# Holding GpSimd's table, row and alibi loads back until the first weight units have landed

## The chip, the cores and the metric

The kernel runs on one core of one Trainium2 chip. The time is the device time of one execution in microseconds (us), and the figure compared is the median of the runs. The core has five engines with a queue of instructions each: TensorE (PE, matmuls and transposes), VectorE (DVE), ScalarE (ACT), GpSimd (POOL) and SyncE (SP, which here only starts DMA transfers). They wait for each other through semaphores, written `wait_ge` in the code.

## The reference

The program is a chain of six stages on 256 tokens of width 1024, all in float32: a hybrid token mixer, a gated FFN, a gMLP mixer, an MLP, a latent attention and a second MLP. The change touches the beginning only:

```python
h = rms_norm(x, mix_pre_norm[l])
mix = hybrid_token_mixer(h, w_in[l], ...)       # proj = h @ w_in; sliding window attention,
                                                # block attention, gated delta rule; @ w_out
x = x + rms_norm(mix, mix_post_norm[l])
```

## The kernel before

All weights stream through SBUF in **units** of 1 MB (128 partitions by 2048 float32). Unit u goes by an SP transfer into one of three `raw` slots (`load`, L169 to L174) and counts on semaphore `landed[u % 3]`. Float32 products are made of three matmuls on a split of each operand into a high and a low part, so a unit is first split: ACT copies `raw` into `w_hi` (`split_hi`, L184), then DVE subtracts to get `w_lo` (`split_lo`, L192) and raises `lo_ready`. A slot is loaded again once `lo_ready` says that its former unit is split. PE uses a unit in 48 matmuls (L202 to L204).

The input X (1 MB, two halves of 512 KB), then units 0, 1 and 2, then ten small parameter transfers (`params_sync`, L253 to L258), then unit 3 and so on are issued by SP in this order. ACT issues the identity matrix and the first gain. GpSimd issues what else the first stage wants: the post-norm row (`rows_load`, 512 KB), mask tables (640 KB), three tiny rows and one 64 KB row (`mix_pool`), all at once at the start, and, when the first norm's transposes are through with the buffer XN, the alibi bias (1 MB, into that same buffer).

The **first norm** goes in halves of the tokens: ACT squares X (L311), DVE adds (L340), GpSimd raises to the power -0.5 (`norm_pool`, L367), ACT and DVE scale (L315, L353), PE transposes into PSUM (L380). PE runs warm-up matmuls on the identity (L289) around this. ACT's queue then has, in order: the copy of the gain (L279), the high half of unit 0 (L184), and the high part of the normalised input hT (L332, eight pieces). DVE's queue has the low half of unit 0 (L192) and then the low part of hT (L359, eight pieces). ACT makes the fifth to eighth high piece only after the first to fourth low piece. PE's first real matmul (L202) needs low unit 0 and the first piece of hT's low part. After that ACT and DVE split units 1 and 2.

`mix_dve` waits for the alibi and for all five small loads at L1734 and L1735, ahead of the first attention scores (L910). The parameters of SP are transposed by PE at the end of unit 3. The post-norm row is used at the end of the stage (`post_dve`).

Of the kernel before, what the change touches and what calls it, by code (L numbers as in the profile page):

```python
# [57 lines left out]
def build(nc, I, out, stages):  # L58

    ctx = ExitStack()  # L60
    with ctx:
# [3 lines left out]
        def sem(name):  # L65
            return ctx.enter_context(nc.semaphore(name))
# [95 lines left out]
        landed = [sem(f"landed{s}") for s in range(RAW)]  # L162
        landed_at = [16 * sum(len(units[v][1]) for v in range(u % RAW, u + 1, RAW)) for u in range(NU)]
# [198 lines left out]
        def norm_pool(pool, n):  # L362
            if n == 0:
                pool.wait_ge(filled, 1)
            for tb in range(TB):
                pool.wait_ge(n_ms, TB * n + tb + 1)
                nc.gpsimd.tensor_tensor(stat[:, 6 + tb:7 + tb], stat[:, 4 + tb:5 + tb], mhalf[:, 0:1],  # L367
                                        ALU.pow).then_inc(n_rstd, 1)
# [47 lines left out]
        def post_pool(pool, q):  # L416
            for tb in range(TB):
                pool.wait_ge(r_ms, TB * q + tb + 1)
                nc.gpsimd.tensor_tensor(stat[:, 14 + tb:15 + tb], stat[:, 12 + tb:13 + tb], mhalf[:, 0:1],
                                        ALU.pow).then_inc(r_rstd, 1)  # L420
# [19 lines left out]
        def rows_load(pool, k, v):  # L440

            if k:
                pool.wait_ge(r_t, 4 * k)
            pool.dma_start(rows[:], v.partition_broadcast(P)).then_inc(rows_in, 16)
# [267 lines left out]
        def gmlp_pool(pool, n):  # L712
            pool.wait_ge(s_mv, TB)
            nc.gpsimd.tensor_scalar(vrs[:, :, 0], mv[:, :, 1], EPS, None, ALU.add).then_inc(s_ve, 1)
            pool.wait_ge(s_ve, 1)
            nc.gpsimd.tensor_tensor(vrs[:, :, 0], vrs[:, :, 0], mhalf[:, 0:TB], ALU.pow).then_inc(s_vr, 1)

        def gmlp_loads(pool, n):
            pool.wait_ge(x_done, 4 * (n - 1))
            pool.dma_start(wsr, I["a_w_s_2"][0].rearrange("g i j -> i g j")).then_inc(s_in, 16)  # L720
            pool.dma_start(lnr[0:GT, :], rowsof(I["a_ln_v_g_2"])).then_inc(s_in, 16)
            pool.dma_start(lnr[GT:2 * GT, :], rowsof(I["a_ln_v_b_2"])).then_inc(s_in, 16)
            pool.dma_start(bsr, I["a_b_s_2"][0].partition_broadcast(P)).then_inc(s_in, 16)
# [329 lines left out]
        def mla_loads(pool, n):  # L1053
            if n > 1:
                pool.wait_ge(x_done, 4 * (n - 1))
            pool.dma_start(mtab, I["table"][:, T_MLA:T_MLA + S + 2]).then_inc(m_in, 16)
            pool.dma_start(posi, I["positions_2"][0].partition_broadcast(P)).then_inc(m_in, 16)

        def mla_pool(pool, n):
            norm_pool(pool, n)  # L1060
            for c, (sq, width) in enumerate(((2, 256), (6, 384))):
                pool.wait_ge(m_sq, sq)
                if c == 0:
                    src = lst[:, 0:2]
                else:
                    nc.gpsimd.tensor_tensor(lst[:, 6:8], lst[:, 2:4], lst[:, 4:6], ALU.add).then_inc(m_p1, 1)
                    pool.wait_ge(m_p1, 2)
                    src = lst[:, 6:8]
                nc.gpsimd.tensor_scalar(lst[:, 8 + 2 * c:10 + 2 * c], src, 1.0 / width, EPS, ALU.mult, ALU.add).then_inc(m_p1, 1)
                pool.wait_ge(m_p1, 1 + 2 * c)  # L1070
                nc.gpsimd.tensor_tensor(lst[:, 12 + 2 * c:14 + 2 * c], lst[:, 8 + 2 * c:10 + 2 * c], mhalf[:, 0:2],
                                        ALU.pow).then_inc(m_rs, 1)
# [287 lines left out]
        def gs_(tb):  # L1360
            return slice(tb * NH, (tb + 1) * NH)
# [44 lines left out]
                at_norm(dve, gs[s - 1])  # L1406

        def mix_pool(pool, n):
            pool.dma_start(msk, I["table"][:, T_TRI:T_MLA].rearrange("p (a b) -> p a b", b=P)).then_inc(d_in, 16)
            pool.dma_start(sinkb, I["swa_sinks"][0].partition_broadcast(P)).then_inc(d_in, 16)  # L1410
            pool.dma_start(alog, I["dn_a_log"][0].partition_broadcast(P)).then_inc(d_in, 16)
            pool.dma_start(dtb, I["dn_dt_bias"][0].partition_broadcast(P)).then_inc(d_in, 16)
            pool.dma_start(dnr[:], I["dn_norm"][0].partition_broadcast(P)).then_inc(d_in, 16)
            norm_pool(pool, n)
            pool.wait_ge(n_tr, 4 * n + 4)
            pool.dma_start(alibi, I["alibi"].rearrange("p (k h s) -> p k h s", k=2, h=NH)).then_inc(d_al, 16)

            for k in range(2):
                c = slice(k * G8, (k + 1) * G8)
                pool.wait_ge(d_ss, 2 * k + 2)  # L1420
                nc.gpsimd.tensor_scalar(sse[:, c], ss[:, c], EPS, None, ALU.add).then_inc(d_se, 1)
                pool.wait_ge(d_se, k + 1)
                nc.gpsimd.tensor_tensor(ri[:, c], sse[:, c], mhalf[:, c], ALU.pow).then_inc(d_ri, 1)

            pool.wait_ge(d_la, 2)
            for lv in range(LEVELS):
                for tb in range(TB):
                    if lv:
                        pool.wait_ge(v_y, 2 * (lv - 1) + tb + 1)
                    if lv == 1:  # L1430
                        pool.wait_ge(v_u, 2 * tb + 2)
                    nc.gpsimd.tensor_tensor(Om[:, gs_(tb), :], Lm[:, gs_(tb), :],
                                            msk[:, 4 + lv, :].unsqueeze(1).to_broadcast([P, NH, P]), ALU.mult).then_inc(v_o, 1)
            pool.wait_ge(f_ss, 2)
            nc.gpsimd.tensor_scalar(ose, oss, 1.0 / DN, EPS, ALU.mult, ALU.add).then_inc(f_se, 1)
            pool.wait_ge(f_se, 1)
            nc.gpsimd.tensor_tensor(ori, ose, mhalf[:, 0:G8], ALU.pow).then_inc(f_ri, 1)
# [426 lines left out]
        posts = [st for st in stages if st in ("mix", "ffn")]  # L1864
        post_rows = {"mix": I["mix_post_norm"][0], "ffn": I["ffn_post_norm"][0]}
# [6 lines left out]
        @block.sync  # L1872
        def _(sp):
            start_sync(sp)
            for n, st in enumerate(stages):
                if st == "ffn":
                    ffn_sync(sp, passes[st])
                elif st.startswith("mlp"):
                    mlp_sync(sp, passes[st], I["mlp_w1_2"][int(st[3])], I["mlp_w2_2"][int(st[3])])
                else:  # L1880
                    for u in range(first_unit[st], last_unit[st] + 1):
                        load(sp, u)
                        if u == RAW - 1:
                            params_sync(sp)
            final_sync(sp)

        @block.gpsimd
        def _(pool):
            for n, st in enumerate(stages):
                if st in posts:  # L1890
                    rows_load(pool, posts.index(st), post_rows[st])
                if st not in ("mix", "mla"):
                    norm_pool(pool, n)
                if st == "mix":
                    mix_pool(pool, n)
                elif st == "gmlp":
                    gmlp_pool(pool, n)
                elif st == "mla":
                    mla_pool(pool, n)
                if "gmlp" in stages[n + 1:n + 2]:  # L1900
                    gmlp_loads(pool, n + 1)
                if "mla" in stages[n + 1:n + 2]:
                    mla_loads(pool, n + 1)
                if st in posts:
                    post_pool(pool, posts.index(st))
            rows_load(pool, len(posts), I["final_norm_g_2"])
            norm_pool(pool, N)
# [140 lines left out]
```

## Time and profile before

| | |
|---|---|
| Median of 3 runs | 1099.99 us (1096.3 to 1104.11) |
| Profiled execution, span from first to last instruction | 1097.3 us |
| PE busy | 1019.0 us (93%) |
| DVE busy | 630.7 us (57%) |
| ACT busy | 496.2 us (45%) |
| POOL busy | 47.5 us (4%) |
| DMA moved | 165.59 MB, mean 151 GB/s |

No time is given for the profiled execution other than its span; the median of the runs is 2.7 us above that span. Engines are PE for matmuls, PEld for PE's weight loads, DVE, ACT, POOL; SPq is the issuing of transfers by SP. L174 is line 174 of the kernel. A time ahead of an instruction is its start in us from the start of the span. The granted TensorE clock is shown as a share of 2.4 GHz, so 0.50 is the level of 1.2 GHz.

### The profile page before, as it was taken

The numbers are of one execution on the slowest core, as the hardware profiler recorded it, in microseconds if no ns is written. First come the engines' busy times: TensorE is split into PE (matmuls) and PEld (weight loads), VectorE is DVE, ScalarE is ACT, GpSimd is POOL, SyncE is SP. The second block draws the span as 40 slices with busy tenths as digits, with TensorE's granted clock in tenths as the row PEclk, the third lists the DMA queues.
The fourth block names the chain that finished last, engine by engine and source line by source line (L and its number), as shares of the span: only waits on it lengthen the run. The fifth ranks groups of instructions, "written<-read, shape, count | busy, mean of one in ns | idle before, by whom it ended". The sixth has DMA issues, their size and how long they took to land.

```text
span 1097.3 us, 16712 instructions
## 1 busy us (share of the span) xinstructions
PE 1019.0 (93%) x6895; PEld 944.5 (86%) x6895; DVE 630.7 (57%) x760; ACT 496.2 (45%) x644; POOL 47.5 (4%) x62
## 2 busy tenths in 40 slices
PE   4989979989999998999998999999889689999997
PEld 4988968779999998998997989999779578899996
DVE  3367664467666666667456655455655536554544
ACT  5355622065445555542445444444554434444442
POOL 1000132020000001000000000000000000000000
PEclk8998969999999999999999999999999799999999
DMA  8542410046555553553554655556444225555550
GB/s 283 155 154 77 154 39 1 1 135 202 184 190 191 191 180 128 158 187 111 195 172 124 218 191 191 191 181 169 137 107 154 77 76 174 192 191 191 180 165 39
DMA packets 131696, 165.59 MB, mean 151 GB/s; under 512 B 23982, under 2 KB 114539, under 8 KB 131515
## 3 DMA queue, kind: packets, MB, share of 16 engines
q1 hardware_dynamic: 130187, 160.10, 45.5%
q0 software_dynamic: 1296, 4.68, 1.4%
q8 instruction: 38, 0.62, 0.2%
q14 instruction: 15, 0.12, 0.0%
q10 hardware_dynamic: 160, 0.07, 0.0%
HBM read 163.78 MB, written 1.05 MB: 150 GB/s over the span
## 4 chain that ended last, share of the span: by engine, by line
PE 84%; DVE 7%; ACT 4%; issue 2%; DMA 1%; POOL 1%; POOLq 0%; SPq 0%; DVEq 0%; ACTq 0%
PE ps L202 26%; PE ps L203 26%; PE ps L204 25%; DMA raw<-in_w_in_dram 1%; DVE w_lo L192 1%; ACT act_tmp L311 1%; ACT w_hi L184 1%; PE ps L1546 1%; PE ps L877 1%; PE ps L1540 1%; PE ps L380 1%; ACT act_tmp L927 1%; PE ps L1551 1%; DVE union L824 1%; PE ps L887 1%
## 5 line engine op out<-in xcount | busy, mean ns | idle before, releaser
L192 DVE TENSOR_TENSOR w_lo<-raw,w_hi 128x2048 fp32r<-128x2048 f32 (+1 forms) x153 | 344.8, 2258 | 199.1 <-ACT w_hi L184 198.1
L202 PE MATMUL ps<-hT_hi,w_hi 128*128 128x256 f32 x1160 | 332.8, 287 | 10.8 <-DVE hT_lo L359 8.2
L184 ACT ACTIVATE w_hi<-raw 128x2048 fp32r<-128x2048 f32 (+1 forms) x153 | 288.6, 1887 | 114.1 <-PE ps L204 107.7
L203 PE MATMUL ps<-hT_hi,w_lo 128*128 128x256 f32 x1160 | 331.1, 285 | 0.0
L204 PE MATMUL ps<-hT_lo,w_hi 128*128 128x256 f32 x1160 | 330.6, 285 | 0.0
L202 PEld LDWEIGHTS ps<-hT_hi,w_hi 128*128 128x128 f32 x1160 | 225.6, 194 | 14.2 <-DVE w_lo L192 8.8
L203 PEld LDWEIGHTS ps<-hT_hi,w_lo 128*128 128x128 f32 x1160 | 225.5, 194 | 1.7
L204 PEld LDWEIGHTS ps<-hT_lo,w_hi 128*128 128x128 f32 x1160 | 225.4, 194 | 0.0
L202 PE MATMUL ps<-w_hi,act_hi 128*128 128x512 f32 x416 | 162.6, 391 | 0.0
L203 PE MATMUL ps<-w_hi,act_lo 128*128 128x512 f32 x416 | 162.4, 390 | 0.0
L204 PE MATMUL ps<-w_lo,act_hi 128*128 128x512 f32 x416 | 161.9, 389 | 0.0
L202 PE MATMUL ps<-w_hi,hT_hi 128*128 128x256 f32 (+3 forms) x320 | 99.1, 310 | 4.1 <-DVE hT_lo L1845 1.6
L203 PE MATMUL ps<-w_hi,hT_lo 128*128 128x256 f32 (+3 forms) x320 | 97.7, 305 | 0.0
L204 PE MATMUL ps<-w_lo,hT_hi 128*128 128x256 f32 (+3 forms) x320 | 97.6, 305 | 0.0
L204 PEld LDWEIGHTS ps<-w_lo,act_hi 128*128 128x128 f32 x416 | 78.1, 188 | 16.6
L202 PEld LDWEIGHTS ps<-w_hi,act_hi 128*128 128x128 f32 x416 | 78.4, 189 | 14.9
L203 PEld LDWEIGHTS ps<-w_hi,act_lo 128*128 128x128 f32 x416 | 78.4, 188 | 14.5
L517 ACT ACTIVATE act_tmp<-ps 128x512 f32<-128x512 f32 x40 | 23.9, 598 | 147.5 <-PE ps L204 147.5
L202 PEld LDWEIGHTS ps<-w_hi,hT_hi 128*128 128x128 f32 x320 | 62.0, 194 | 8.2 <-issue 2.1
L203 PEld LDWEIGHTS ps<-w_hi,hT_lo 128*128 128x128 f32 x320 | 62.2, 194 | 2.8 <-issue 0.2
L204 PEld LDWEIGHTS ps<-w_lo,hT_hi 128*128 128x128 f32 x320 | 62.0, 194 | 2.7
L626 DVE SCALAR_TENSOR_TENSOR act_tmp<-ps,par,act_tmp 128x255 f32<-128x255 f32 (+1 forms) x88 | 36.4, 476 | 36.1 <-ACT act_tmp L596 36.1
(270 smaller groups left out, 918.7 us busy)
## 6 DMA issues: line engine op xcount, KB each, us to landing
raw<-in_mlp_w_dram SPq DMA_DIRECT2D x64, 1024.0 KB, 5.4
raw<-in_w_up_dram SPq DMA_DIRECT2D x22, 1024.0 KB, 5.1
raw<-in_a_w_in_dram SPq DMA_DIRECT2D x16, 1024.0 KB, 5.5
raw<-in_w_in_dram SPq DMA_DIRECT2D x12, 1024.0 KB, 6.4
raw<-in_w_down_dram SPq DMA_DIRECT2D x11, 1024.0 KB, 4.9
raw<-in_a_w_out_dram SPq DMA_DIRECT2D x8, 1024.0 KB, 5.0
raw<-in_w_out_dram SPq DMA_DIRECT2D x4, 1024.0 KB, 4.9
raw<-in_b_w_o_dram SPq DMA_DIRECT2D x4, 1024.0 KB, 4.9
```

Of the source, the lines that this page charges most:

```text
L184: nc.scalar.activation(w_hi[:, s, 0:n], raw[:, r, 0:n], ACT.Copy).then_inc(hi_ready, 1)
L192: nc.vector.tensor_tensor(w_lo[:, s, 0:n], raw[:, r, 0:n], w_hi[:, s, 0:n].bitcast(F32), ALU.subtract).then_inc(lo_ready, 1)
L202: nc.tensor.matmul(o, a[0], b[0], start=start, stop=False)
L203: nc.tensor.matmul(o, a[1], b[0], start=False, stop=False)
L204: return nc.tensor.matmul(o, a[0], b[1], start=False, stop=stop)
L311: nc.scalar.activation(act_tmp[:, b, :], half(b), ACT.Square, scale=D ** -0.5, accum_out=stat[:, b:b + 1]).then_inc(n_sq, 1)
L380: mm = pe.transpose(turned(t)[:, tb * P:(tb + 1) * P], XN[:, tb, t * P:(t + 1) * P], ident[:])
L517: nc.scalar.activation(act_tmp[:, m, :], W[m][:], func).then_inc(f.t, 1)
L626: nc.vector.scalar_tensor_tensor(ys, bank[:, t * S:(t + 1) * S - back], conv_taps(j, half, t, 2 - back), ys, ALU.mult, ALU.add).then_inc(d ...
L824: nc.vector.scalar_tensor_tensor(svT[:, t, :].rearrange("p (b i) -> p b i", b=TB), ACC[t // 2 % 4][:, t % 2 * S:(t % 2 + 1) * S].rearrange ...
L877: mm = nc.tensor.matmul(o, qs[m], ks[m], start=m == 0, stop=m == len(qs) - 1)
L887: tr = pe.transpose(ACC[kb][:, h * P:(h + 1) * P], pr[:, h, kb * P:(kb + 1) * P], ident[:])
```

## The change

GpSimd now does the power step of the first norm ahead of all its loads. It then waits until unit 1 has landed and issues the table, the three tiny rows and the 64 KB row; it waits until unit 2 has landed (and, as before, until the transposes are done) and issues the alibi and, after it, the post-norm row. The loads themselves, and everything on the other engines, are the same.

```diff
         def mix_pool(pool, n):
+            norm_pool(pool, n)
+            pool.wait_ge(landed[1], landed_at[1])
             pool.dma_start(msk, I["table"][:, T_TRI:T_MLA].rearrange("p (a b) -> p a b", b=P)).then_inc(d_in, 16)
             pool.dma_start(sinkb, I["swa_sinks"][0].partition_broadcast(P)).then_inc(d_in, 16)
             pool.dma_start(alog, I["dn_a_log"][0].partition_broadcast(P)).then_inc(d_in, 16)
             pool.dma_start(dtb, I["dn_dt_bias"][0].partition_broadcast(P)).then_inc(d_in, 16)
             pool.dma_start(dnr[:], I["dn_norm"][0].partition_broadcast(P)).then_inc(d_in, 16)
-            norm_pool(pool, n)
+            pool.wait_ge(landed[2], landed_at[2])
             pool.wait_ge(n_tr, 4 * n + 4)
             pool.dma_start(alibi, I["alibi"].rearrange("p (k h s) -> p k h s", k=2, h=NH)).then_inc(d_al, 16)
+            rows_load(pool, 0, post_rows["mix"])
...
         @block.gpsimd
         def _(pool):
             for n, st in enumerate(stages):
-                if st in posts:
-                    rows_load(pool, posts.index(st), post_rows[st])
+                if st == "ffn":
+                    rows_load(pool, 1, post_rows[st])
                 if st not in ("mix", "mla"):
                     norm_pool(pool, n)
```

## Rows read from the trace of the kernel before

**Rows 1.** The page's head.
```profile
span 1097.3 us, 16712 instructions
```

**Rows 2.** The chain that ended last, 0 to 260 us: start, length, what.
```profile
1.65 14.69 DMA raw<-in_w_in_dram
16.36 1.92 ACT w_hi L184
...
21.14 0.55 PE ps L202
...
64.65 0.69 DVE act_tmp L910
```

**Rows 3.** Timeline, 0 to 24 us: start, length, engine, line, tiles, count, idle before.
```profile
4.84 0.63 ACT L311 ACTIVATE act_tmp<-X 128x512 f32<-128x512 f32 x1 [1.76 <-DMA X<-in_x_dram]
...
6.52 0.56 POOL L367 TENSOR_TENSOR stat<-stat,mhalf 128x1 f32<-128x1 f32 x1 [1.91 <-DVE stat L340]
...
9.31 0.72 ACT L315 ACTIVATE XN<-X,stat 128x512 f32<-128x512 f32 x1 [0.86 <-POOL stat L367]
...
9.94 0.15 ACT L279 COPY par<-ps 128x8 f32<-128x8 f32 x1
...
11.48 0.59 POOL L1416 DMA_DIRECT2D XN<-in_alibi_dram  x1 [2.20 <-PE ps L380]
...
18.31 2.29 DVE L192 TENSOR_TENSOR w_lo<-raw,w_hi 128x2048 fp32r<-128x2048 f32 x1 [8.51 <-ACT w_hi L184]
...
20.51 3.22 DVE L359 SCALAR_TENSOR_TENSOR hT_lo<-ps,par,hT_hi 128x256 fp32r<-128x256 f32 x8
...
21.53 0.40 SPq L174 DMA_DIRECT2D raw<-in_w_in_dram  x1
```

**Rows 4.** Timeline of ACT, 24 to 64 us (first row: from 22.58).
```profile
22.58 3.91 ACT L184 ACTIVATE w_hi<-raw 128x2048 fp32r<-128x2048 f32 x2
29.13 0.59 ACT L1618 COPY union<-ps 128x512 f32<-128x512 f32 x1 [2.65 <-PE ps L204]
...
34.89 1.18 ACT L1628 COPY union<-ps 64x512 f32<-64x512 f32 x2 [3.36 <-PE ps L204]
```

**Rows 5.** DMA issues, 0 to 8 us: count, size of each, median us to landing.
```profile
raw<-in_w_in_dram SPq DMA_DIRECT2D x3, 1024.0 KB, 19.7
```

**Rows 6.** DMA queues, 0 to 5 us: packets, MB, share (SP's and ACT's queue).
```profile
q1 hardware_dynamic: 237, 0.91, 53.8%
```

**Rows 7.** DMA queues, 6 to 8 us; q0 is GpSimd's.
```profile
q1 hardware_dynamic: 135, 0.14, 22.0%
q0 software_dynamic: 138, 0.54, 78.0%
```

**Rows 8.** DMA queues, 0 to 120 us.
```profile
q0 software_dynamic: 560, 2.30, 6.4%
```

**Rows 9.** Windows: from:to, length, busy PE PEld DVE ACT POOL (count), granted clock, DMA share, GB/s.
```profile
3.00:5.00 2.00, 0.00 (x0) 0.00 (x0) 0.00 (x0) 0.24 (x2) 1.61 (x4) 1.00 0.98 343
10.00:11.00 1.00, 0.91 (x8) 0.92 (x9) 0.00 (x0) 0.09 (x2) 0.00 (x0) 1.00 0.86 99
13.42:15.40 1.98, 0.00 (x0) 0.00 (x0) 0.00 (x0) 0.00 (x0) 0.00 (x0) 1.00 1.10 395
21.14:25.66 4.52, 4.52 (x21) 4.52 (x22) 3.75 (x8) 4.43 (x6) 0.00 (x0) 0.50 0.94 292
101.33:103.45 2.12, 0.01 (x1) 0.01 (x1) 1.40 (x2) 2.10 (x8) 0.00 (x0) 1.00 0.06 23
104.15:107.60 3.45, 3.45 (x19) 3.45 (x18) 3.10 (x7) 3.42 (x4) 0.00 (x0) 0.51 0.00 0
219.64:221.20 1.56, 0.00 (x0) 0.00 (x1) 1.29 (x2) 1.56 (x3) 0.00 (x0) 1.00 0.02 5
```

**Rows 10.** Timeline, 904.5 to 907.5 us.
```profile
905.58 0.68 POOL L444 DMA_DIRECT2D rows<-in_final_norm_g_dram  x1
905.66 0.72 ACT L315 ACTIVATE XN<-X,stat 128x512 f32<-128x512 f32 x1 [0.86 <-POOL stat L367]
905.66 0.49 DVE L353 TENSOR_SCALAR XN<-X,stat 128x512 f32<-128x512 f32 x1 [0.67 <-POOL stat L367]
```

## The prediction

> **What bounds the kernel now.** The page's head gives a span of 1097.3 us [rows 1], and I read the start through the chain that ended last, since the change moves nothing after it. The chain begins with one transfer: unit 0, issued at 1.65 us, and ACT splits it at 16.36 [rows 2]. PE's first real matmul comes at 21.14 [rows 2], 4.78 us later: high half 1.92, low half 2.29, first low piece of hT, hand-overs. From there it runs on PE; so a us saved before 21.14 is a us of the kernel, unless a later load or split cannot follow.
>
> The timeline shows that the norm is not what holds this. GpSimd's power step at 6.52 waited 1.91 us for DVE, idle from its loads by then, and ACT scaled the second half at 9.31 and copied the gain at 9.94 [rows 3]. ACT was free at 10.09 and stood until 16.36, 6.3 us, for unit 0.
>
> Now whose bytes were in the way. Up to 5 us SP's and ACT's queue had moved 0.91 MB at a total rate of 343 GB/s, and no byte of GpSimd's appears [rows 6, 9]. From 6 to 8 us GpSimd's queue took 0.54 MB and SP's 0.14 [rows 7]: weights crept at a fifth of the traffic. At 10 us the total itself fell to 99 GB/s [rows 9]. The three first units took 19.7 us in the median to land [rows 5].
>
> **The change part by part.**
>
> *The power step ahead of the loads*: nothing. It waited for DVE, not for the loads [rows 3]. X's landing gains nothing either, as GpSimd's bytes start only after 5 us, and X's first half was there at 4.84 [rows 3, 6]. Bounds: 0 to 1.76 us (ACT's whole wait for X [rows 3]) gained; I take 0.
>
> *Unit 0 without GpSimd's bytes.* The queue must move X and unit 0, 2.10 MB. 0.91 is done at 5.0 us; the other 1.19 at 343 GB/s take 3.5 us, to 8.5. With some 0.6 us for the tail, an estimate, unit 0 lands at about 9.1, while ACT is busy until 10.09. One us of cover. The late bound: the queue stays at half that rate, then 12.0. By the same rate unit 1 lands at about 12.2 and unit 2 at 15.2.
>
> *ACT's split of unit 0 then follows the gain copy.* It starts at 10.1 in place of 16.36, and PE starts 4.78 us later, at 14.9. The high pieces of hT go beside DVE's 2.29. Gain: 21.14 - 14.9 = **6.2 us**.
>
> *The clock.* PE's warm-up ended at 13.42; the clock stayed at 2.4 GHz for 1.98 us and fell at 15.40 to 1.2 GHz, at which PE did its first 21 matmuls in 4.52 us, 0.215 each [rows 9]. With a start at 14.9 PE stands 1.5 us. Of the gaps later in the trace, one of 1.56 us kept the clock and one of 2.12 us was followed by 3.45 us at half speed [rows 9]. 1.5 is nearest to 1.56, so I take it that the clock is kept.
>
> *Unit 0's matmuls.* Before: 21.14 to 29.1, where ACT takes the result [rows 4], 8.0 us. After: the first 24 matmuls are fed by DVE's eight low pieces, 3.22 us [rows 3]; a matmul at full clock takes (34.89 - 29.13) / 48 = 0.12 us [rows 4], so 2.9 for the other 24. PE ends unit 0 at 14.9 + 3.2 + 2.9 = 21.0. That is 8.1 us before 29.1: **1.9 us more** than the start alone.
>
> *Units 1 and 2.* DVE's low pieces run from about 14.3 to 17.5 and ACT's last high piece ends at 16.3. High half 1.92 to 18.2, low half 2.29 to 20.5: ready 0.5 us before PE wants it at 21.0. Unit 2 follows at 22.8, wanted at 26.8. Nothing lost; if the clock is kept and the cover of 0.5 is gone, DVE's split is late next.
>
> *The added waits.* Behind GpSimd's wait for unit 1 stand six loads and nothing that another engine needs soon; its next compute comes over 100 us later. Five loads at 0.6 us each [rows 3] run from 12.2 to 15.2, then alibi and row. First use is DVE's L910 at 64.65 [rows 2], 56.5 after the change. The parameter transfers of SP are wanted after unit 3, at about 38 us. The row waits for the end of the stage.
>
> *Unit 3 beside the held-back loads.* This is where their bytes now go. GpSimd's queue carries 2.30 MB in all [rows 8]; unit 3 and the parameters are 1.19. All 3.5 MB at 343 GB/s from 14.7 us end at 24.9, so unit 3 lands by 25.5 at the latest (before it was issued at 21.53 [rows 3]; now it may go when unit 0 is split, 14.3, after SP's ten small issues). PE wants it after units 0 to 2 at 21.0 + 2 * 5.76 = 32.5; less 4.2 for the two halves, at 28.3. Cover 2.8 us, cost 0.
>
> A rule speaks against the change. The Trainium skill (DMA: Bandwidth & Descriptors, Rules for kernel authors) would have a DMA issued early and waited for late. By that rule holding loads back can only expose them; the first rows show the other side, a load nobody wants for 40 us in front of one that everybody wants. By the rule the sum would be 0 or a loss.
>
> Sum: -6.2 - 1.9 = -8.1, span 1089.2. The median stands 2.7 above the profiled span, so 1100.0 - 8.1 = **1091.9 us**.
>
> **The rivals.**
>
> *Clock lost at the restart.* The fall may come at 15.4 all the same, or after PE has resumed: after the gap of 2.12 us it came 0.7 us into the matmuls [rows 9]. A spell of 3.45 us at half speed takes 0.64 us per three matmuls; five groups go in it, the other eleven at 0.36 need 3.9, and unit 0 ends at about 22.3, not 21.0. Gain 6.8: 1093.2. A second spell takes it to 5: 1095. For it: 1.98 is not far from 1.5. Against: the gap of 1.56.
>
> *Unit 0 lands late.* The queue of SP could be slow by itself, since its 0.91 MB by 5 us are mostly X, in other packets than the units. At the late bound of 12.0, ACT starts 1.9 us later, PE at 16.8 after 3.4 us of idleness, longer than both gaps that lost the clock. Unit 0 ends about as far from the start as before: gain 4.3, 1095.7. If GpSimd's bytes were no hindrance at all, landing and time stay: 1100. Against this last: 0.14 of 0.68 MB [rows 7].
>
> *GpSimd and DVE get in each other's way.* The five issues of 0.6 us now fall into DVE's low half of unit 0 (12.0 to 14.3), on the path. In rows of before, an issue of 0.68 us beside a DVE operation left it at 0.49 us, and that is the nearest case [rows 10]; none has L192 in it. Price at worst all five, 3.0 us late, with the clock lost: gain 3.2, 1096.8. The Trainium skill (SBUF — State Buffer, Who interferes with whom) speaks of an exclusive port pair that DVE with two SBUF inputs and GpSimd contend for; rows 10 don't show such a block.
>
> *Slower: the held-back loads choke unit 3.* Place: 15 to 25 us. It decides from the point where unit 3 lands after 28.3, and eats the whole gain at 36.4. If the mixture with the tiny rows kept the traffic at the 99 GB/s of 10 us [rows 9], 3.5 MB need 35 us, unit 3 lands at 50, PE waits 21.7 us: -8.1 + 21.7 = +13.6, 1113.6. Against: by 13.42 the traffic was back at 395 GB/s, with the alibi's bytes in it [rows 9].
>
> *More than forecast.* Later clock spells fall elsewhere when the start moves; each is worth about 1.5 us (3.45 us at half speed). Two fewer make -11.1, 1088.9. Two more would make -5.1.
>
> **How the numbers follow.** Forecast 0.42; clock lost 0.22; unit 0 late 0.13; no effect 0.06; DVE and GpSimd 0.05; choked unit 3 0.03; two spells or more fewer 0.09. The runs of before span 7.8 us, so I give a median of three 2 to 3 us either way; 1% (11.0 us) is about what a measurement of this kernel can tell from no change. Faster by over 1% is under 1089.0: most of the 0.09, a fourth of the forecast's 0.42 and a little of the clock case, 0.22. Slower by over 1%: 0.04. Within: 0.74. Range 1086.5 to 1099: below it some of the spell case, above it no effect and the choke.
>
> **What would show it.** Unit 0 at ACT (L184) at about 10.1 with the gain copy, not the DMA, before it; PE's L202 at 14.9; granted clock 1.00 from 13 to 21 us; ACT's first L1618 at 21.0; no idle PE at units 1 to 3; L910 at 56.5 without waiting for a load. Wrong it would be if L184 still waits for the DMA past 11, if L192 takes more than 2.29, or if PE stands before unit 3.

## The result and the profile after

| | before | after |
|---|---|---|
| Median | 1098.45 us (13 runs, 1095.5 to 1104.11) | 1091.22 us (13 runs, 1088.14 to 1096.37) |
| Profiled span | 1097.3 us | 1091.0 us |

The ratio is 0.9932, with a 95% interval of 0.9917 to 0.9948: 0.7% or 7.5 us faster (5.7 to 9.1 us by the interval). The forecast was 1091.9 us, a change within 1%.

The timeline of the changed kernel from 0 to 24 us answers to [rows 3] (start, length, engine, line, tiles, count, idle before; the line numbers of the changed kernel are up to three higher):

```profile
5.09 0.63 ACT L311 ACTIVATE act_tmp<-X 128x512 f32<-128x512 f32 x1 [2.01 <-DMA X<-in_x_dram]
...
6.77 0.55 POOL L367 TENSOR_TENSOR stat<-stat,mhalf 128x1 f32<-128x1 f32 x1 [6.32 <-DVE stat L340]
...
10.16 0.14 ACT L279 COPY par<-ps 128x8 f32<-128x8 f32 x1
10.21 1.92 ACT L184 ACTIVATE w_hi<-raw 128x2048 fp32r<-128x2048 f32 x1
...
12.15 2.29 DVE L192 TENSOR_TENSOR w_lo<-raw,w_hi 128x2048 fp32r<-128x2048 f32 x1 [2.13 <-ACT w_hi L184]
12.68 0.70 POOL L1411 DMA_DIRECT2D union<-in_table_dram  x1 [3.18 <-DMA raw<-in_w_in_dram]
...
14.36 3.22 DVE L359 SCALAR_TENSOR_TENSOR hT_lo<-ps,par,hT_hi 128x256 fp32r<-128x256 f32 x8
...
15.81 0.54 POOL L1418 DMA_DIRECT2D XN<-in_alibi_dram  x1 [0.27 <-DMA raw<-in_w_in_dram]
```

ACT's high half of unit 0 now has no idle time before it and begins at 10.21, behind the gain copy, not at 16.36 behind a transfer. DVE's low half takes 2.29 us, as before, although GpSimd issues three loads beside it (at 12.68, 13.37 and 13.92). PE's first real matmul comes at 14.99:

```profile
14.99 0.36 PE L202 MATMUL ps<-hT_hi,w_hi 128*128 128x256 f32 x1 [1.35 <-DVE hT_lo L359]
```

Here the gap of PE is 1.35 us. The windows of the changed kernel (busy times of PE, PEld, DVE, ACT, POOL, then granted clock, DMA share, GB/s) show that the clock was kept through it, and what comes later:

```profile
13.64:15.00 1.36, 0.01 (x1) 0.04 (x1) 1.36 (x3) 0.13 (x1) 1.36 (x4) 1.00 1.16 346
50.00:60.00 10.00, 10.00 (x48) 10.00 (x48) 4.16 (x2) 2.65 (x4) 0.00 (x0) 0.50 0.53 172
60.00:130.00 70.00, 62.15 (x508) 59.88 (x507) 49.16 (x83) 42.55 (x86) 4.04 (x4) 0.97 0.38 121
```

The same stretches of the kernel before:

```profile
50.00:60.00 10.00, 10.00 (x89) 10.00 (x87) 4.58 (x2) 4.47 (x4) 0.00 (x0) 0.99 0.34 107
60.00:130.00 70.00, 63.91 (x491) 61.94 (x492) 45.40 (x78) 38.90 (x80) 0.00 (x0) 0.90 0.37 121
```

So the changed kernel ran 10 us at half speed from 50 us on. Before lost its clock in the same unit 5, but only at its end, and for 3.3 us (59.8 to 63.1):

```profile
59.00:60.00 1.00, 1.00 (x10) 1.00 (x10) 0.62 (x1) 0.00 (x0) 0.00 (x0) 0.88 0.03 4
60.00:61.00 1.00, 1.00 (x6) 1.00 (x7) 0.00 (x0) 0.59 (x2) 0.00 (x0) 0.50 0.29 34
```

The changed kernel made up for it later (0.97 against 0.90 from 60 to 130 us). ACT's timeline of the changed kernel, 18 to 57 us, answers to [rows 4]:

```profile
21.18 0.59 ACT L1621 COPY union<-ps 128x512 f32<-128x512 f32 x1 [1.05 <-PE ps L204]
29.15 1.91 ACT L184 ACTIVATE w_hi<-raw 128x2048 fp32r<-128x2048 f32 x1 [7.39 <-DMA raw<-in_w_in_dram]
30.97 1.16 ACT L1631 COPY union<-ps 64x512 f32<-64x512 f32 x2
33.48 1.92 ACT L184 ACTIVATE w_hi<-raw 128x2048 fp32r<-128x2048 f32 x1 [1.35 <-DMA raw<-in_w_in_dram]
...
41.93 0.37 ACT L1623 COPY union<-ps 64x256 f32<-64x256 f32 x1 [5.77 <-PE ps L204]
...
47.98 0.58 ACT L1621 COPY union<-ps 128x512 f32<-128x512 f32 x1 [3.11 <-PE ps L204]
...
56.10 0.17 ACT L1638 COPY dd<-ps 128x16 f32<-128x16 f32 x1 [5.44 <-PE ps L204]
```

Read as a ledger against before, with the first post-norm square at the end of the mixer as a last mark:

| ACT's copy after | before | after | difference |
|---|---|---|---|
| unit 0 | 29.13 | 21.18 | -7.95 |
| unit 3 | 48.84 | 41.93 | -6.91 |
| unit 4 | 54.90 | 47.98 | -6.92 |
| unit 5 | 60.41 | 56.10 | -4.31 |
| end of the mixer (L413) | 229.0 | 222.7 | -6.3 |
| span | 1097.3 | 1091.0 | -6.3 |

The start gives 8.0 us. One us is lost between units 0 and 3, where ACT waited 7.39 us for unit 3 and PE waited for its split (PE's waits, 14 to 62 us: line, what for, us in total, times, longest):

```profile
PE ps L202 <- DVE w_lo L192: 0.8, 1, 0.8
```

Another 2.6 us go in unit 5, where the clock falls early; 2.0 of these come back by the end of the mixer. This ledger is of one profiled execution of each kernel; which part of it holds in the median is what the experiments ask.

### The profile page after: what moved, and what is told of

Its sections match the earlier page's. It is cut to its first block, busy times and chain, and to the rows that moved or that the text cites. A ratio compares the mean times of both kernels' runs of the same rounds, so it can differ in the third digit from the quotient of the medians.

```text
span 1091.0 us, 16713 instructions
## 1 busy us (share of the span) xinstructions
PE 1018.0 (93%) x6895; PEld 942.8 (86%) x6895; DVE 630.5 (58%) x760; ACT 495.1 (45%) x644; POOL 47.5 (4%) x62
## 4 chain that ended last, share of the span: by engine, by line
PE 84%; DVE 7%; ACT 4%; issue 2%; DMA 2%; POOL 1%; POOLq 0%; DVEq 0%
PE ps L202 26%; PE ps L203 25%; PE ps L204 25%; DMA raw<-in_w_in_dram 1%; DVE w_lo L192 1%; ACT act_tmp L311 1%; PE ps L877 1%; ACT w_hi L184 1%; PE ps L1549 1%; PE ps L1543 1%; PE ps L380 1%; PE ps L1554 1%; ACT XN L315 1%; DVE union L824 1%; POOL stat L367 1%
## 5 line engine op out<-in xcount | busy, mean ns | idle before, releaser
L192 DVE TENSOR_TENSOR w_lo<-raw,w_hi 128x2048 fp32r<-128x2048 f32 (+1 forms) x153 | 344.6, 2256 | 194.8 <-ACT w_hi L184 193.8
```

Of the source, the lines that this page charges most:

```text
L192: nc.vector.tensor_tensor(w_lo[:, s, 0:n], raw[:, r, 0:n], w_hi[:, s, 0:n].bitcast(F32), ALU.subtract).then_inc(lo_ready, 1)
```

## The experiments

### The order alone

All waits for weight units are left out; GpSimd does the power steps first and then issues its loads. The edit against the kernel before, in which the row stood at the head of the queue:

```diff
         def mix_pool(pool, n):
+            norm_pool(pool, n)
+            rows_load(pool, 0, post_rows["mix"])
             pool.dma_start(msk, ...)
             ...
-            norm_pool(pool, n)
             pool.wait_ge(n_tr, 4 * n + 4)
```

> Only the order is changed: GpSimd does the first norm's two power steps ahead of its loads, with no wait for a weight unit. In the trace of the changed kernel the second step ends at 9.5 us, so this order alone moves the loads from 1.2 us to 9.5 us. Theory of the bytes (what matters is whose bytes are ahead of unit 0, whose own last byte comes at about 8.5 us): unit 0 lands at 9.4 us as in the changed kernel, PE starts at 15.0, and the time is within 1.5 us of the changed kernel's, some 6 to 7.5 us under before; the two waits add nothing to the start. Rival (the waits for the units are what brings the gain): unit 0 lands after 12 us, and the time is within 3 us of before. Rival (the norm's place matters by itself): the first power step is earlier than 6.5 us; the theory of the bytes has it at 6.5 to 6.8.

1089.22 us, ratio 0.9923 (0.9898 to 0.9947). GpSimd's timeline in this kernel:

```profile
8.95 0.55 POOL L367 TENSOR_TENSOR stat<-stat,mhalf 128x1 f32<-128x1 f32 x1 [1.64 <-DVE stat L340]
9.45 0.70 POOL L444 DMA_DIRECT2D rows<-in_mix_post_norm_dram  x1
```

and ACT's:

```profile
10.20 1.91 ACT L184 ACTIVATE w_hi<-raw 128x2048 fp32r<-128x2048 f32 x1
...
21.36 1.91 ACT L184 ACTIVATE w_hi<-raw 128x2048 fp32r<-128x2048 f32 x1 [3.04 <-DMA raw<-in_w_in_dram]
```

Unit 0 is there in time, as in the changed kernel; unit 2 is late at ACT (3.04 us of waiting, at 21.36), but not for PE: the copy after unit 3 came at 40.88. In this profile the clock fell only at 52.2 us, for 3.4 us, and the mixer ended at 218.1 (229.0 in the kernel before). The waits for units 1 and 2 bring nothing that can be measured. It is enough that the loads stand behind the norm.

### The waits, with the power steps behind them

Against the changed kernel, the power steps go back behind the first five loads:

```diff
         def mix_pool(pool, n):
-            norm_pool(pool, n)
             pool.wait_ge(landed[1], landed_at[1])
             ...
+            norm_pool(pool, n)
             pool.wait_ge(landed[2], landed_at[2])
```

> The waits for units 1 and 2 stay, but the power steps stand behind the five first loads, as they stood before. Theory: the power step now waits for unit 1 (12.4 us) and five issues (to 15.5 us); then half a norm, the gain copy and the high half of unit 0 follow one after the other, hi at about 19.3, PE's first real matmul at about 24 us, 3 us later than before the change, with the clock lost, so the time is 2 to 4 us over before. Rival (the move of the power step is only order and costs or gives nothing): the time is that of the changed kernel, 7 us under before.

1099.51 us, ratio 1.0009 (0.9992 to 1.0025): nothing left of the gain. The power step and what followed it:

```profile
15.27 0.59 POOL L367 TENSOR_TENSOR stat<-stat,mhalf 128x1 f32<-128x1 f32 x1
...
18.75 1.91 ACT L184 ACTIVATE w_hi<-raw 128x2048 fp32r<-128x2048 f32 x1
```

PE's timeline:

```profile
20.62 3.38 PE L289 MATMUL ps<-ident 128*128 128x128 f32 x20
23.75 0.36 PE L202 MATMUL ps<-hT_hi,w_hi 128*128 128x256 f32 x1
```

The first real matmul came at 23.75, as expected. That the clock would be lost was wrong: the warm-up moves with the transposes (it ran from 20.62), so PE entered unit 0 at full speed and ended it at 29.8, 0.7 us after before, not 3. The expected 2 to 4 us over before did not come either. The move of the power steps is thus a condition of the change.

### All loads held until unit 3 has landed

Against the changed kernel:

```diff
-            pool.wait_ge(landed[1], landed_at[1])
+            pool.wait_ge(landed[0], landed_at[3])
...
-            pool.wait_ge(landed[2], landed_at[2])
```

> The changed kernel, but all of GpSimd's loads are held until unit 3 has landed. In the changed kernel unit 3 took 14.7 us to land (29.1 us), 0.8 us later than PE's need allows, and ACT stood 7.4 us for it and 1.4 us for unit 4. Theory of the collision: with nothing of GpSimd's beside it unit 3 lands at 20 to 21 us, PE has no wait before unit 3, the copy after it comes at 40.9 us in place of 41.9, and the time is 1.0 us under the changed kernel, 8 to 9 under before. Unit 4, issued at about 20.7 us, now meets the 2.3 MB; it may land up to 36 us without cost. Rival (unit 3 is slow for SP's own small parameter transfers): it still lands after 26 us. Rival (the stall is only moved): unit 4 or 5 lands late, PE waits there, and the time is that of the changed kernel.

1090.96 us, ratio 0.9928 (0.9911 to 0.9946). ACT's timeline:

```profile
20.84 0.59 ACT L1620 COPY union<-ps 128x512 f32<-128x512 f32 x1 [1.04 <-PE ps L204]
21.32 1.91 ACT L184 ACTIVATE w_hi<-raw 128x2048 fp32r<-128x2048 f32 x1
...
36.03 1.91 ACT L184 ACTIVATE w_hi<-raw 128x2048 fp32r<-128x2048 f32 x1 [8.26 <-DMA raw<-in_w_in_dram]
...
40.55 0.37 ACT L1622 COPY union<-ps 64x256 f32<-64x256 f32 x1 [1.84 <-PE ps L204]
```

Unit 3 landed by 19.8 us and ACT no longer waits for it; now unit 4 meets GpSimd's 2.3 MB and lands at 36.0, just within what PE allows. The copy after unit 3 stands at 40.55, 1.4 us earlier than in the changed kernel; 0.3 of these were there at unit 0 already. So without GpSimd's loads beside it unit 3 costs nothing, and the price of the collision in the changed kernel was 1.0 us (one profile of each kernel; PE's wait for the split of unit 3 is gone too). In the median it doesn't show, and the clock fell in unit 5 here too.

### The clock alone

Against the kernel before, the warm-up matmuls behind the first norm are made 40:

```diff
                 if n == 0:
-                    warm(pe, 10)
+                    warm(pe, 40)
```

> The kernel before with 40 warm-up matmuls behind the first norm in place of 10, which fill PE's idle time up to about 20.6 us; no load and no wait is changed. Theory of the clock: the granted clock stays at 1.00 up to PE's first real matmul at 21.1 us; the 21 matmuls that took 0.215 us each then go at the pace of DVE's low pieces or 0.12, unit 0 ends at 27.3 and not at 29.1, and the time is 1.8 us under before: of the change's gain 1.9 us is the clock's and 6.2 the landing's. Rival (the clock costs nothing there, DVE is the bound in any case): 0. Rival (the clock falls later anyway in the same place): the spell at half speed is in the trace after 21 us and the gain is under 0.5 us.

1099.26 us, ratio 0.9993 (0.9975 to 1.001). Windows, and ACT's copies after units 0, 4 and 5:

```profile
13.00:21.00 8.00, 7.70 (x69) 7.51 (x68) 2.69 (x3) 3.37 (x5) 0.00 (x0) 1.00 1.04 371
50.00:55.00 5.00, 5.00 (x46) 5.00 (x44) 2.29 (x1) 1.90 (x2) 0.00 (x0) 1.00 0.29 75
55.00:60.00 5.00, 5.00 (x28) 5.00 (x27) 2.29 (x1) 0.77 (x2) 0.00 (x0) 0.56 0.59 178
```
```profile
27.32 0.59 ACT L1618 COPY union<-ps 128x512 f32<-128x512 f32 x1 [0.16 <-PE ps L204]
...
53.10 0.58 ACT L1618 COPY union<-ps 128x512 f32<-128x512 f32 x1 [3.12 <-PE ps L204]
...
60.75 0.17 ACT L1635 COPY dd<-ps 128x16 f32<-128x16 f32 x1 [4.97 <-PE ps L204]
```

Locally the term is exact: unit 0 ends 1.8 us earlier (29.13 to 27.32) with PE starting at 21.14 as before, and the 1.8 us are still there after unit 4 (54.90 to 53.10). After unit 5 they are gone (60.41 to 60.75): the clock fell within that unit. The median is within its interval of both 0 and -1.8 us, so whether the clock's part of the gain reaches the end was not settled by the time.

### Unit 5 widened, with and without the change

Unit 5 is 48 matmuls of 8 columns each, in which the clock fell in before, in the changed kernel and in the four-fold warm-up. Here it takes 128 columns, of which ACT copies the last 8; its load grows from 32 to 512 KB with it.

```diff
-                unit(cols(w_in, 3328, 8, 0, 8))
+                unit(cols(w_in, 3208, 128, 0, 128))
...
-                    c0, width = {5: (0, 8), 3: (P, P)}.get(k, (0, UC))
+                    c0, width = {5: (0, P), 3: (P, P)}.get(k, (0, UC))
...
-                    nc.scalar.copy(ba, bank[:, 0:16].rearrange(...))
+                    nc.scalar.copy(ba, bank[:, 0:2 * P].rearrange(...)[:, :, P - 8:P])
```

> The changed kernel with unit 5 widened: its 48 matmuls take 128 columns (of which the last 8 are the ones wanted) in place of 8; the unit's load grows from 32 KB to 512 KB. In the traces of before, of the changed kernel and of the three kernels run with it, PE is busy without a gap in unit 5's 8-column matmuls and yet the granted clock falls there: at 59.8 us in before, at 50.0 us in the changed kernel, where it then stays at 0.50 for 10.2 us and 48 matmuls stand where 89 stood. Theory (narrow matmuls are what the clock falls on, and part of the gain at the start is given back in this place): with 128 columns the matmuls keep their 0.11 to 0.12 us, the clock stays at 1.00 from 45 to 62 us, unit 5's copy comes 5.5 us after unit 4's as in before (60.4 - 54.9) and not 8.1 (56.1 - 48.0), and the time is 2 to 5 us under the changed kernel. Rival (the clock falls for another reason at about this time): the spell stays and the time is the changed kernel's. Rival (the larger load and splits cost what is won): ACT or DVE is late for unit 6 and PE stands.

1089.53 us, ratio 0.9915 (0.9893 to 0.9937).

> The kernel before with the same widened unit 5 and nothing else. Theory: before lost less there (clock down at 59.8 us, some 6 us at half speed around unit 5 and 6), so this brings 1 to 3 us; and between this kernel and the changed kernel with the same wide unit the whole 6.9 to 8 us of the start are left, since nothing in this place gives them back. Rival (the clock falls for another reason): time of before.

1096.19 us, ratio 0.9982 (0.9968 to 0.9995). Windows of the changed kernel with the wide unit:

```profile
45.00:50.00 5.00, 5.00 (x46) 5.00 (x45) 1.78 (x2) 2.62 (x3) 0.00 (x0) 1.00 0.44 134
50.00:55.00 5.00, 5.00 (x46) 5.00 (x46) 2.33 (x2) 2.06 (x3) 0.00 (x0) 1.00 0.59 170
```

The clock stays at 1.00. Unit 5's copy comes 5.4 us after unit 4's (52.75 - 47.38), as expected; with 8 columns at full clock it came 5.3 us after (52.25 - 46.94 in the order-alone kernel). So 48 matmuls of 128 columns take about as long as 48 of 8. Over all kernels of this document: in the nine with 8 columns the clock fell in unit 5, between 2 us after its start and its last matmul; in the four with 128 columns it stayed at 1.00 through it. The rival (the clock falls at about this time for another reason) does not fit that. The larger load came with the columns in every case, so no run separates the two. On the kernel before the edit is worth 0.18% (2 us). On the changed kernel 0.9915 against 0.9932 points the same way, but the intervals overlap. And between the two kernels with the wide unit the change is worth 0.9915 / 0.9982 = 0.9933, the same as without it: in the median, unit 5 gives back nothing of this change in particular. My expectation of 2 to 5 us on the changed kernel, drawn from one profile with a spell of 10.2 us, was narrowly missed (1.9 us by the ratios, 1.7 by the medians). The one for the kernel before, 1 to 3 us, was met.

### Which of the early loads held unit 0 back

From the kernel before, first the alibi alone is held until unit 2 has landed; then also the three tiny rows and the 64 KB row are issued behind it.

```diff
             norm_pool(pool, n)
+            pool.wait_ge(landed[2], landed_at[2])
             pool.wait_ge(n_tr, 4 * n + 4)
             pool.dma_start(alibi, ...)
+            # second kernel only: sinkb, alog, dtb, dnr are issued here, not ahead of norm_pool
```

> The kernel before with one edit: the alibi load waits for unit 2 to have landed; row, table and small rows are issued at the start as before. By bytes: of GpSimd's 1.57 MB moved up to 16.3 us some 0.33 MB are the alibi's, so without them unit 0 lands 1 us earlier, 15.3 us. Theory of the order (it is the loads issued at 1 to 4 us that delay unit 0): 14.5 to 15.5 us. Rival (the alibi, whose 1 MB meets the tail of unit 0, is the main hindrance): unit 0 lands under 13 us.

1097.81 us, ratio 0.9994 (0.9975 to 1.0013).

> As the kernel with the late alibi, and the three tiny rows and the 64 KB row are issued after the alibi too; only post-norm row and table (1.15 MB) stay at the start. Theory of the tiny rows: they move 70 KB in all, but in every trace the total rate falls to 99 to 228 GB/s where they are in flight (10 to 12 us in before, 16 to 22 us in the changed kernel). Without them 2.10 + 1.2 MB at 343 GB/s end at 11.9 us, and unit 0 lands at 12 to 13 us. Theory of the bytes alone (70 KB is nothing): the landing is that of the kernel with the late alibi, 14.5 to 15.5 us.

1095.77 us, ratio 0.9976 (0.9956 to 0.9997). ACT's high half of unit 0 and the window 9 to 12 us, with the alibi alone late:

```profile
16.14 1.91 ACT L184 ACTIVATE w_hi<-raw 128x2048 fp32r<-128x2048 f32 x1 [6.03 <-DMA raw<-in_w_in_dram]
```
```profile
9.00:12.00 3.00, 2.46 (x23) 2.23 (x22) 0.49 (x1) 0.77 (x2) 0.30 (x1) 1.00 1.03 179
```

and with the small rows late as well:

```profile
12.35 1.91 ACT L184 ACTIVATE w_hi<-raw 128x2048 fp32r<-128x2048 f32 x1 [2.37 <-DMA raw<-in_w_in_dram]
```
```profile
9.00:12.00 3.00, 2.56 (x22) 2.32 (x21) 0.49 (x1) 0.77 (x2) 0.17 (x1) 1.00 1.07 367
```

The alibi (1 MB) was worth 0.2 us and not the 1 us expected; the four small rows, 70 KB, were worth 3.8 us. That is far above the scatter of this mark: in three kernels with all the early loads it stood at 16.36, 16.37 and 16.45. The DMA share is full in both windows (1.03 and 1.07), but the rate halves, 179 against 367 GB/s, where the small rows are in flight. The queues of the first trace show how: from 8 to 9 us, 67 packets of GpSimd's queue with 0.34 MB took 82% of the time of the 16 DMA engines, 0.20 us each; from 9 to 12 us, when 119 of all packets were under 512 bytes, 147 packets of this queue with only 0.15 MB took 64%, 0.21 us each. In these two windows the queue's packets took the same time at 5 KB and at 1 KB on average. Those of SP's queue took 0.05 us in both kernels. The 2.4 us that ACT still waited are, by subtraction, the row and the table, since the order alone, which moves these too, leaves no wait. Of the 6.3 us that ACT stood for unit 0, the small rows made more than half.

At the end of unit 4 the second kernel is 3.5 us ahead of before (51.39 against 54.90), after unit 5 only 1.0 us (59.42 against 60.41), since its clock fell at 53.5; its median is 2.6 us under before by the ratio.

### The small rows last, in the changed kernel

Against the changed kernel:

```diff
+            pool.wait_ge(landed[0], landed_at[3])   # behind the post-norm row
+            pool.dma_start(sinkb, ...)              # and alog, dtb, dnr, from behind the table
```

> The changed kernel with the three tiny rows and the 64 KB row taken out of the place behind the table and issued last, once unit 3 has landed; table, alibi and post-norm row as in the changed kernel. In the kernel before, the same move of the same 70 KB brought unit 0 from 16.1 to 12.35 us. Theory of the tiny rows: they are what held unit 3 back too, so it lands at 24.5 to 26 us and not at 29.15, before PE's need of 28.3; the copy after unit 3 comes at 41 us in place of 41.9, 1 us gained at this place. Theory of the bytes alone (my prediction's sum, 3.5 MB at one rate): nothing changes, 29 us. In the median both lie within 1.5 us of the changed kernel.

1091.14 us, ratio 0.9924 (0.9903 to 0.9945). ACT's timeline and the window 16 to 22 us:

```profile
24.81 1.91 ACT L184 ACTIVATE w_hi<-raw 128x2048 fp32r<-128x2048 f32 x1 [3.29 <-DMA raw<-in_w_in_dram]
...
40.64 0.37 ACT L1624 COPY union<-ps 64x256 f32<-64x256 f32 x1 [5.21 <-PE ps L204]
```
```profile
16.00:22.00 6.00, 6.00 (x51) 6.00 (x51) 5.22 (x6) 4.47 (x4) 0.74 (x2) 1.00 1.04 369
```

The changed kernel in the same window:

```profile
16.00:22.00 6.00, 6.00 (x51) 6.00 (x50) 5.22 (x7) 4.71 (x5) 0.89 (x2) 1.00 0.98 214
```

Unit 3 lands at 24.8 instead of 29.1, with the table, alibi and post-norm row as they were; 369 GB/s instead of 214. PE no longer waits before unit 3, and the copy after it comes 1.3 us earlier (40.64 against 41.93; 0.25 of these were there at unit 0 already). The large loads cost unit 3 time as well (24.8 against 19.8 with nothing of GpSimd's beside it), but inside its cover; it is the small rows that took it past. The median is that of the changed kernel, as expected.

### Towards a better version

The order alone with the wide unit (the edits of the first and fifth experiment together):

> The order alone (norm's power steps ahead of the loads, no wait for a weight unit) with the widened unit 5. The order alone stood at 0.9923 of before, the changed kernel at 0.9932, the changed kernel with the wide unit at 0.9915. Theory (the waits add nothing, the wide unit is worth about 2 us on either): 0.990 to 0.992. Rival (the waits are worth something once the clock does not blur it): over 0.993.

1088.95 us, ratio 0.9911 (0.9891 to 0.9931). The waits for the units again add nothing. In its trace unit 3 reached ACT at 29.15 and PE waited 1.0 us for its split, where the first experiment, with the same loads in the same order up to unit 4, had it at 27.36 and no wait. So the order alone did not keep unit 3 in time in both; whether the larger load of unit 5 has a part in the 1.8 us is not shown.

All loads held until unit 3, the small rows last, the wide unit:

> The candidate for the best: all of GpSimd's loads held until unit 3 has landed, the tiny rows last, and unit 5 widened. Unit 3 should land at 20 us, unit 4 in time, no wait of PE before unit 5, the clock at 1.00 from 45 to 62 us. Theory (the pieces add): 1.0 us for unit 3 and 1.9 us for the wide unit beside the changed kernel's 0.9932, so 0.990 to 0.991, 1088.5 to 1089.5 us. Rival (unit 4, 5 or the alibi is late): PE stands before unit 4 or DVE's first attention scores, and it is no better than 0.9915.

1088.79 us, ratio 0.9906 (0.9884 to 0.9929), the lowest of all, as forecast. Its trace has unit 3 landed by 19.9, no wait of PE up to unit 5, and the clock at 1.00 from 45 to 60 us. Its interval overlaps the changed kernel's (0.9917 to 0.9948), so that it beats before is shown, and that it beats the changed kernel is likely only. The tidy separate gains of 1.0 and 1.9 us would take 0.9932 to 0.9906.

## Why the prediction was right, point by point

- **Power step ahead, 0 us.** As an operation, yes: it ended its wait for DVE at 6.77. But I costed it as a step that moves alone. With nothing else changed it moves the loads behind it from 1.24 to 9.45 us, and the first experiment shows that this is the whole gain. The right number came by charging it all to the waits: the mechanism (loads out of unit 0's way) holds, the part of the diff to which I gave it does not.
- **Unit 0 at about 9.1, under cover of ACT until 10.09.** It landed 7.7 us after its issue at 1.65, at 9.35; units 1 and 2 freed GpSimd at 12.68 and 15.81 (forecast 12.2 and 15.2). The total rate of 343 GB/s held (347 from 13 to 15 us).
- **Start of PE at 14.9.** 14.99. Gain 6.15 of 6.2.
- **Clock kept.** Granted clock 1.00 across a gap of 1.35 us. The rival of the lost clock falls in this profile and in those of the six other kernels that start at about 15 us (gaps of 0.9 to 1.4 us, clock 1.00 up to 20 us). The price of the lost clock is confirmed by the longer warm-up (1.8 us for the whole effect, forecast 1.9). The choice itself rested on one gap of 1.56 us.
- **Unit 0 ends at 21.0.** Copy at 21.18, 7.95 us earlier; forecast 8.1.
- **First attention scores at 56.5.** L910 came at 60.3, without waiting for a load: unit 3 and the spell in unit 5 held it up.
- **GpSimd against DVE.** L192 took 2.29 us beside three issues, and not five as forecast, and L359's eight pieces 3.22 beside the next ones, as in [rows 3]. The Trainium skill (SBUF — State Buffer, Who interferes with whom) names an exclusive port pair for DVE with two SBUF inputs and a GpSimd operation that reads SBUF; the page infers that descriptor writing is spared, and this trace agrees: 0 us.
- **Unit 3 beside the held-back loads, cost 0.** This step was mis-sized. I let all 3.5 MB flow at 343 GB/s and had unit 3 by 25.5. It landed at 29.1, 0.8 past the 28.3 that PE's need allows, and cost 1.0 us; PE stood 0.8 us before unit 3, one of the prediction's own signs of being wrong. The rate fell to 214 GB/s from 16 to 22 us, for the small rows, which I had counted by their bytes; I had seen 99 GB/s at 10 us in [rows 9] and used it for the slower rival only. With them away unit 3 lands at 24.8, before the 25.5 that I had given. The rival of the choked unit 3 had the right place and the wrong size: 1.0 us and not 21.7.
- **Causes in before.** I laid the delay of unit 0 on bytes ahead of it (0.54 of 0.68 MB from 6 to 8 us). Large loads made the smaller part; of 6.3 us, 3.8 came from 70 KB.
- **Spells of the clock, 1.5 us each.** By its own rows the price should have been 1.7, half of 3.45. A long spell arose in units 5 and 6 (0.50 from 50 to 60 us), and from 60 to 130 us the mean clock was 0.97 against 0.90, which is 70 * 0.07 / 0.5 = 9.8 us less at half speed. The sum came out near 0 in this profile, so the gain stayed inside the bounds of -11.1 and -5.1. Why the later spells fall where they do is open.
- **What was luck.** The span moved by 6.3 us and the median by 7.2 to 7.5, not 8.1. The forecast was counted from 1100.0, the median of three runs; that of thirteen is 1098.45, from which the same sum gives 1090.4. So the base was 1.5 us too high and the gain about 1 us too large, and the two made up for each other. The 1.0 us lost at unit 3 was in no term of the sum, and the early spell in unit 5 only in its bounds; without what came back later, the profile would have shown 4.3 us.
- **The early-issue rule.** The Trainium skill (DMA: Bandwidth & Descriptors, Rules for kernel authors) has a DMA issued early. Here the measurement decides against it: the same loads issued 8 us later, behind the power steps and with no wait added, made the kernel 8.5 us faster (ratio 0.9923; 5.8 to 11.2 us by its interval), since nobody wanted them before 56 us and unit 0 was wanted at 10.

## What to carry to other kernels

Order the first loads by who needs them first; a load that nobody wants for 40 us belongs behind the one that starts TensorE. Here it was enough to put it behind an early compute step on its own queue; with the waits, but with that step behind the loads, the gain was gone. Count small rows by their packets, not by their bytes, and look for stretches where the DMA share is full and the rate low. Before calling a gain at the start whole, follow it through a ledger of marks (the copy after each unit): a local gain of 1 to 2 us (the longer warm-up, unit 3 in time) did not show in the median here, where the clock falls in one place or another.

## What the runs showed of the hardware

- **Tiny rows cost far over their size.** Three loads of 16 bytes to each of 128 partitions (2 KB each) and one of 512 bytes (64 KB) halve the total rate, or nearly, for some 3 to 6 us: 179 against 367 GB/s from 9 to 12 us, 214 against 369 from 16 to 22 us. They made a 1 MB weight load land 3.8 and 4.3 us later. The Trainium skill (DMA: Bandwidth & Descriptors, Specifications) gives 512 B as the least transfer at line rate, with read-modify-write below. The traces agree with it in direction; no run separates the three 16-byte loads from the 512-byte one.
- **A busy TensorE can lose its clock.** In 48 matmuls of 8 columns with no gap between them, the granted clock fell from 2.4 to 1.2 GHz in all nine kernels that have them (at 50.0 us in the changed kernel, at 59.8 in before); in the four with 128 columns it stayed at 2.4 GHz, and the 48 matmuls took about as long (5.4 us against 5.3). What in the wider unit keeps the clock was not separated further.
- **Late is not lost.** A late unit costs nothing until its cover ends: unit 2 came 3.0 us late to ACT in the order-alone kernel and unit 4 8.3 us late in the held kernel, both without a wait of PE. Unit 3, 0.8 us past its cover in the changed kernel, cost 1.0 us.
